# Closing norm of a two-layer decoder step: row sums on TensorE, one store queue

## The chip, the cores and the metric

One core of a Trainium2 chip runs the whole kernel. The metric is the device time of one launch in microseconds (us), as the median of several runs; lower is better. The engines are TensorE (PE, its weight loads listed apart as PEld), VectorE (DVE), ScalarE (ACT), GpSimd (POOL) and SyncE (SP, which only issues transfers here).

## The reference, cut to what matters

The kernel computes one inference step of a two-layer decoder for 256 prompt tokens and 64 sample tokens (8 sequences of 8), with 1024 features each: attention, then gated linear attention, each followed by a mixture of 64 experts. What the change touches is the very last step, after the experts of layer 1:

```python
x = x + g2 * moe(hffn, ...)
return rms_norm(x, final_g), ...

def rms_norm(x, g):
    y = xf * lax.rsqrt(jnp.mean(xf * xf, axis=-1, keepdims=True) + NORM_EPS)
    return (y * g).astype(x.dtype)
```

So each of the 320 tokens needs the sum of its 1024 squares, one root, one reciprocal, and then a product with its own factor and with the row `final_g`. The outputs are `y_prompt` (256 x 1024, float32) and `y_sample` (64 x 1024).

## The kernel before, in words

The residual stream x is kept in on-chip memory as `xT`, features on partitions: 8 chunks (`KC`) of 128 features by 320 tokens. Tokens come in three tiles (`TILES`): 128 prompt tokens, 128 more, and the 64 sample tokens. The expert sums `acct` have tokens on partitions, so at the end of a layer they are turned back chunk by chunk.

The closing stage is `final` (L2218), called from `moe` at L2145. Its PE program (L2233 to L2245) runs over the chunks m = 0 to 7. `back` (L2153) turns chunk m of `acct` with two transposes (L2165) into the one bank of PSUM or the other; at m = 0 and m = 4 `back_sample` (L2147) turns the sample tokens of four chunks first (L2150). `gated_back` on DVE (L2168) multiplies by the gate and adds to `xT` (L2179; for the sample tokens L2174 and L2177), and counts up `x_full`. Behind the `back` of chunk m, PE runs `turned(m - 1)` (L2235): three transposes (L2238), one a tile, which turn the finished chunk so that tokens are on partitions, in the two-bank tensors `ybank`, `pair[1]` and `pair[0]`. The order on PE is thus back 0, back 1, turned 0, back 2, turned 1 and so on to back 7, turned 6, turned 7. `back` of chunk m waits for x of chunk m - 2 (it writes the bank that DVE read), `turned(m)` for x of chunk m.

When four chunks are turned, ACT squares each tile's half and sums it along the row in the same instruction (L2256, two halves by three tiles, the result in `stt`). After the second half DVE adds the two halves (L2270), ACT takes the root (L2259), DVE the reciprocal (L2272). Then three tiles go three ways. Tile 0: one DVE instruction scales by the token's factor and by `g_row` (L2275), and SP stores it (L2291). Tile 2, the sample tokens: ACT scales it (L2263), POOL multiplies by `g_row` (L2283) and issues its store (L2285). Tile 1: ACT scales it behind tile 2 (L2263), DVE multiplies by `g_row` (L2277), SP stores it (L2291). SP then waits for its two stores, POOL for its own.

`g_row` was loaded long before, through the ring of weight slots (L301). The helper `sums` of the other norms of the kernel (L344) sums squares over partitions by products with `ones`, with a 32-column block of ones as the stationary operand. `ada_fold` (L508) and the router (L1602) are other places of the kernel that the prediction takes durations from, and so are the product of two expert-sum parts (L1132), the attention's transposes (L693), the squares of the other norms (L342) and the subtraction at L2108.

## Time and profile before

| | before |
|---|---|
| median of 3 runs | 1496.29 us (1495.95 to 1497.87) |
| the profiled execution, its own time | 1501.47 us |
| its span in the trace | 1499.9 us |
| PE busy | 1443.8 us, 96% of the span, 8392 instructions |
| DVE busy | 439.0 us, 29% |
| ACT busy | 322.0 us, 21% |
| POOL busy | 50.7 us, 3% |
| share of PE in the chain that ended last | 92% |
| TensorE clock granted, mean | 0.985 of full |
| read and written over the span | 499.16 MB and 11.01 MB |

Times inside the trace are counted from the start of the span. A product of two float32 operands shows as two instructions of PE (and two weight loads), a transpose as one. PE's instructions are pipelined, so their listed durations overlap; what one costs in a row of its like is the distance of the starts. In the notation of a PE row, `128*64 128x128` is a stationary operand of 128 partitions by 64 columns and a moving one of 128 by 128.

### The profile page before, as it was taken

To read this page: it belongs to the slowest core of one execution; us is meant where nothing else is said; L and a number is where in the kernel's file an instruction comes from. 1 tells how busy PE (TensorE), PEld (TensorE's weight loads), DVE (VectorE), ACT (ScalarE), POOL (GpSimd) and SP (SyncE) were. 2 spreads that over 40 slices of the span, in tenths; PEclk is the share of its full clock that TensorE was granted. 3 is DMA by queue.
4 is the path that set the end of the run, shared out by engine and by line. 5 is a ranking of instruction groups with operands and counts; after the bars stand their busy time and mean duration, and the time that the engine had idled before them with its cause. 6 is when DMAs were issued, how large, how long until landed. Compare 5 with 4: busy or idle time off the path is not lost.

```text
span 1499.9 us, 21008 instructions
## 1 busy us (share of the span) xinstructions
PE 1443.8 (96%) x8392; PEld 729.0 (49%) x8392; DVE 439.0 (29%) x1146; ACT 322.0 (21%) x752; POOL 50.7 (3%) x86
## 2 busy tenths in 40 slices
PE   6998999999999999999999999999999999999996
PEld 2344666544444445444465455564444454444443
DVE  2126525221221312221352243442122212222113
ACT  3024414111111111111262222321111111111113
POOL 0100302000000000000100010010000000000000
PEclk9999999999999999999999997999999999999998
DMA  9878506999999999999952252189999999999991
GB/s 399 358 309 363 212 14 242 426 377 428 423 423 427 425 424 425 426 424 425 426 230 80 112 208 87 49 346 403 404 423 425 423 427 426 424 426 426 424 419 51
DMA packets 47459, 509.61 MB, mean 340 GB/s; under 512 B 5728, under 2 KB 6000, under 8 KB 8160
## 3 DMA queue, kind: packets, MB, share of 16 engines
q1 hardware_dynamic: 26352, 364.33, 58.3%
q10 hardware_dynamic: 17280, 125.84, 20.3%
q0 software_dynamic: 3728, 18.07, 3.2%
q8 instruction: 69, 1.13, 0.3%
q14 instruction: 30, 0.25, 0.0%
HBM read 499.16 MB, written 11.01 MB: 340 GB/s over the span
## 4 chain that ended last, share of the span: by engine, by line
PE 92%; ACT 3%; DVE 2%; DMA 2%; issue 1%; ACTq 0%; SPq 0%; DVEq 0%
PE bank L1933 27%; PE banks L1982 14%; PE banks L1835 10%; PE banks L430 5%; PE ybank L1863 4%; PE banks L1072 4%; PE banks L1863 3%; PE bank L1865 3%; PE bank L491 2%; PE banks L673 2%; PE banks L1100 2%; DMA s_gu_ring<-in_ada_w_dram 2%; PE ybank L1627 1%; PE banks L1627 1%; PE banks L1077 1%; PE bank L1959 1%
## 5 line engine op out<-in xcount | busy, mean ns | idle before, releaser
L1933 PE MATMUL bank<-s_gu_ring,s_hbuf 128*32 128x512 f32 (+1 forms) x2752 | 409.4, 593 | 0.9 <-DVE s_hbuf L2063 0.9
L1933 PEld LDWEIGHTS bank<-s_gu_ring,s_hbuf 128*32 128x32 f32 (+1 forms) x2752 | 127.4, 119 | 273.6 <-issue 273.6
L1982 PE MATMUL banks<-s_dn_ring,s_hTs 128*32 128x512 f32 (+1 forms) x1376 | 211.5, 596 | 3.8 <-issue 3.8
L2108 DVE TENSOR_TENSOR s_ylo<-banks,s_yhi 128x512 fp32r<-128x512 f32 x116 | 80.2, 692 | 334.6 <-ACT s_yhi L2024 334.6
L1835 PE MATMUL banks<-s_sel,s_htok 128*128 128x512 f32 (+2 forms) x640 | 149.2, 381 | 0.5 <-issue 0.5
L1835 PEld LDWEIGHTS banks<-s_sel,s_htok 128*128 128x128 f32 x640 | 109.9, 188 | 60.7 <-issue 44.4
L2024 ACT CAST s_yhi<-banks 128x512 fp32r<-128x512 f32 x116 | 68.0, 586 | 308.5 <-PE banks L1982 308.5
L1982 PEld LDWEIGHTS banks<-s_dn_ring,s_hTs 128*32 128x32 f32 (+1 forms) x1376 | 58.8, 119 | 125.4 <-issue 125.4
L2103 DVE SCALAR_TENSOR_TENSOR s_hh<-s_sg,s_wsl,bank 128x256 f32<-128x256 f32 x58 | 27.9, 480 | 298.6 <-ACT s_sg L2015 298.6
L2015 ACT ACTIVATE s_sg<-bank 128x256 f32<-128x256 f32 x58 | 22.3, 385 | 376.8 <-PE bank L1933 376.8
L2063 DVE COPY s_hbuf<-banks 128x512 f32<-128x512 f32 (+1 forms) x60 | 40.4, 674 | 100.4 <-PE banks L1835 100.4
L1072 PE MATMUL banks<-s_gu_ring,s_hbuf 128*128 128x512 f32 x128 | 55.9, 593 | 0.5 <-DVE s_rs L1366 0.5
L1998 ACT COPY s_hbuf<-banks 128x512 f32<-128x512 f32 (+1 forms) x60 | 34.4, 573 | 60.1 <-PE banks L1835 60.1
L673 PE MATMUL banks<-s_gu_ring,s_hbuf 128*128 128x512 f32 x96 | 42.4, 597 | 1.2 <-DMA s_gu_ring<-in_wqkv_dram 1.2
L1863 PE MATMUL ybank<-s_yhi,s_gt 128*128 128x512 f32 x112 | 40.1, 438 | 0.0
L430 PE MATMUL banks<-s_qk,s_gu_ring 128*128 128x320 f32 x128 | 38.1, 462 | 1.0 <-ACT s_qk L1303 1.0
L1072 PEld LDWEIGHTS banks<-s_gu_ring,s_hbuf 128*128 128x128 f32 x128 | 24.2, 191 | 29.1 <-issue 28.2
L430 PE MATMUL banks<-s_hbuf,s_gu_ring 128*128 128x320 f32 x128 | 37.4, 456 | 0.8 <-DVE s_hbuf L969 0.8
L491 PE MATMUL bank<-s_gu_ring,s_condT 128*32 128x512 f32 x256 | 34.6, 666 | 2.5 <-DMA s_gu_ring<-in_ada_w_dram 2.5
L2019 ACT COPY s_hTs<-bank 128x256 f32<-128x256 f32 x58 | 21.6, 373 | 68.7 <-PE bank L1959 47.0
L1863 PE MATMUL ybank<-s_ylo,s_gt 128*128 128x512 f32 x112 | 35.4, 397 | 0.0
L1863 PE MATMUL banks<-s_yhi,s_gt 128*128 128x512 f32 x112 | 35.2, 395 | 0.0
(423 smaller groups left out, 1460.2 us busy)
## 6 DMA issues: line engine op xcount, KB each, us to landing
s_gu_ring<-in_moe_up_dram SPq DMA_DIRECT2D x128, 2048.0 KB, 17.5
s_dn_ring<-in_moe_wd_dram ACTq DMA_DIRECT2D x120, 1024.0 KB, 17.6
s_gu_ring<-in_ada_w_dram SPq DMA_DIRECT2D x24, 2048.0 KB, 14.1
s_gu_ring<-in_win_dram SPq DMA_DIRECT2D x6, 2048.0 KB, 15.3
s_dn_ring<-in_moe_wd_dram SPq DMA_DIRECT2D x8, 1024.0 KB, 19.2
s_gu_ring<-in_wqkv_dram SPq DMA_DIRECT2D x3, 2048.0 KB, 21.7
s_gu_ring<-in_wo_dram SPq DMA_DIRECT2D x2, 2048.0 KB, 12.3
s_gu_ring<-in_shared_up_dram SPq DMA_DIRECT2D x2, 2048.0 KB, 12.8
```

The lines of the kernel that those rows point to most:

```text
L430: last = pe.matmul(b[:, 0:T], item(slot)[:, k, (m % 4) * P:(m % 4 + 1) * P], src[:, k, :], start=(k == 0), stop=(k == KC - 1))
L491: last = pe.matmul(ada_bank(n)[32 * j:32 * j + 32, :], condT[:, k, lo:lo + 32], item(s)[:, k, :], start=(x == 0 and kk == 0), stop=(ends_g ...
L673: last = pe.matmul(b[:, :], hT[:, k, t0:t0 + P], item(slots[cch])[:, k, :], start=(k == 0), stop=(k == KC - 1))
L1072: last = pe.matmul(b[:, :], hT[:, k, t0:t0 + P], w[:, k, :], start=(k == 0), stop=(k == KC - 1))
L1835: last = pe.matmul(b[:, width * x:width * x + width], w[:, m * P:(m + 1) * P], sel[:, s, 0:width], start=(n == 0), stop=(n == 4))
L1863: last = pe.matmul(acc[(t, half)], g[:, t * P:(t + 1) * P], y[:, half, :], start=(p == 0 and y is yhi), stop=False)
L1865: last = pe.matmul(bank[6][:, :], g[:, 320 - 64 * half:448 - 64 * half], y[:, half, :], start=(p == 0 and y is yhi and half == 0), stop=False)
L1933: last = pe.matmul(W0[o:o + n, :], tokens_of(p, k)[:, o:o + n], w[:, k, :, :], start=(k == 0), stop=(k == KC - 1))
L1982: last = pe.matmul((W1, W2)[half][o:o + n, :], hTs[:, f, o:o + n], dn_ring[:, dn_of[(l, r)][0], w0:w0 + 512], start=(f == 0), stop=(f == 1))
L2024: act.copy(yhi[:, half, :], (W1, W2)[half]).then_inc(S["y_high"], 1)
L2063: dve.tensor_copy(fill_target(q, f), fill_source(q, f)).then_inc(S["fill_dve"], 1)
L2108: dve.tensor_tensor(ylo[:, half, :], (W1, W2)[half], yhi[:, half, :].bitcast(F32), ALU.subtract).then_inc(S["y_low"], 1)
```

## The change

In `final`, the squares and their sums move. ACT now squares each chunk of `xT` as soon as x of that chunk is there (8 instructions of 128x320), into a buffer `sq` that lies in the first two slots of the ring of down weights. PE sums the squares over the partitions: for each chunk and tile one float32 product with the squares as the stationary operand (128x128, or 128x64 for the sample tokens) and one column of ones as the moving operand, which leaves one column for each chunk in PSUM. These products are put into PE's loop ahead of back 3 (chunk 0), back 5 (chunks 1 and 2) and back 7 (chunks 3 and 4), and between turned 6 and turned 7 (chunks 5, 6 and 7). DVE adds up the eight columns (two reductions, one for the two prompt tiles, one for the sample tile). On tile 1 the product with `g_row` comes first, in two halves, the first behind the last x and the second behind turned 7; ACT then scales it from on-chip memory. Tile 2 is done by DVE in one instruction behind tile 0. SP issues all three stores, in the order tile 0, tile 1, tile 2. POOL has no work left here, and the clearing of `stt` at L2267 is gone.

```diff
-                    final(c, l, i, acct, gate)
+                    old_down = dn_ring[:, 0:2, :].rearrange("p s n -> p (s n)")
+                    final(c, l, i, acct, gate, old_down[:, 0:KC * T].rearrange("p (k t) -> p k t", t=T))
...
+            row_sum = bank[6][:, 256:256 + 3 * KC].rearrange("p (t m) -> p t m", m=KC)
...
+                def row_sums(m):
+                    pe.wait_ge(N["sq_full"], KC * i + m + 1)
+                    for t, (t0, tn) in enumerate(TILES):
+                        last = pe.matmul(row_sum[0:tn, t, m:m + 1], sq[:, m, t0:t0 + tn], ones[:, 0:1], start=True, stop=True)
+                    return last
+
                 for m in range(KC):
+                    if m in (3, 5, 7):
+                        pe.wait_ge(N["x_full"], KC * (i - 1) + m - 1)
+                        for k in range(max(m - 4, 0), m - 2):
+                            row_sums(k)
                     back(pe, l, i, acct, m)
                     if m:
                         turned(m - 1)
+                pe.wait_ge(N["x_full"], KC * i)
+                row_sums(5)
+                row_sums(6)
+                row_sums(7).then_inc(N["sum_psum"], 1)
                 turned(KC - 1)
...
             @block.scalar
             def _(act):
                 act.activation(spare[:, i:i + 1], cc("eps"), ACT.Sqrt)
-                for half in range(2):
-                    act.wait_ge(E["x_psum"], 4 * (half + 1))
-                    for t, (t0, tn) in enumerate(TILES):
-                        n = 3 * half + t
-                        if n >= 2:
-                            act.wait_ge(N["sq_full"], KC * i + n - 1)
-                        act.activation(junk[0:tn, n % 2, :], out[t][0:tn, half, :], ACT.Square,
-                                       accum_out=stt[0:tn, half, t:t + 1]).then_inc(N["sq_full"], 1)
+                for m in range(KC):
+                    act.wait_ge(N["x_full"], KC * (i - 1) + m + 1)
+                    act.activation(sq[:, m, :], xT[:, m, :], ACT.Square).then_inc(N["sq_full"], 1)
                 act.wait_ge(N["part_full"], i + 1)
-                act.activation(stt[:, 3, :], stt[:, 2, :], ACT.Sqrt, scale=1.0 / D, bias=cc("eps")).then_inc(N["root_full"], 1)
+                act.activation(stt[:, 0, 0:2], stt[:, 0, 0:2], ACT.Sqrt, scale=1.0 / D, bias=cc("eps")).then_inc(N["root_full"], 1)
+                act.wait_ge(N["part_full"], i + 2)
+                act.activation(stt[0:NS, 0, 2:3], stt[0:NS, 0, 2:3], ACT.Sqrt, scale=1.0 / D, bias=cc("eps")[0:NS, :]).then_inc(N["root_full"], 1)
+                act.wait_ge(E["gained"], 1)
                 act.wait_ge(N["rstd_full"], i + 1)
-                for t in (2, 1):
-                    tn = TILES[t][1]
-                    act.activation(yt[0:tn, t, :], flat_out(t), ACT.Copy, scale=stt[0:tn, 2, t:t + 1]).then_inc(E["scaled"], 1)
+                act.activation(yt[:, 1, :], yt[:, 1, :], ACT.Copy, scale=stt[:, 1, 1:2]).then_inc(E["scaled"], 1)
 
             @block.vector
             def _(dve):
-                dve.memset(stt[:, :, :], 1.0).then_inc(E["y_full"], 1)
                 gated_back(dve, l, gate, add)
-                dve.wait_ge(N["sq_full"], KC * i + 6)
-                dve.tensor_tensor(stt[:, 2, :], stt[:, 0, :], stt[:, 1, :], ALU.add).then_inc(N["part_full"], 1)
+                slot_in[g_slot].wait(dve, g_in)
+                dve.wait_ge(E["x_psum"], KC // 2)
+                dve.tensor_tensor(yt[:, 1, 0:512], out[1][:, 0, :], g_row[:, 0:512], ALU.mult)
+                dve.wait_ge(N["sum_psum"], 2 * i + 1)
+                dve.tensor_reduce(stt[:, 0, 0:2], row_sum[:, 0:2, :], AX.X, ALU.add).then_inc(N["part_full"], 1)
+                dve.tensor_reduce(stt[0:NS, 0, 2:3], row_sum[0:NS, 2:3, :], AX.X, ALU.add).then_inc(N["part_full"], 1)
+                dve.wait_ge(E["x_psum"], KC)
+                dve.tensor_tensor(yt[:, 1, 512:1024], out[1][:, 1, :], g_row[:, 512:1024], ALU.mult).then_inc(E["gained"], 1)
                 dve.wait_ge(N["root_full"], i + 1)
-                dve.reciprocal(stt[:, 2, :], stt[:, 3, :]).then_inc(N["rstd_full"], 1)
+                dve.reciprocal(stt[:, 1, 0:2], stt[:, 0, 0:2]).then_inc(N["rstd_full"], 1)
+                dve.wait_ge(N["root_full"], i + 2)
+                dve.reciprocal(stt[0:NS, 1, 2:3], stt[0:NS, 0, 2:3]).then_inc(N["rstd_full"], 1)
                 dve.wait_ge(N["rstd_full"], i + 1)
-                slot_in[g_slot].wait(dve, g_in)
-                dve.scalar_tensor_tensor(yt[:, 0, :], flat_out(0), stt[:, 2, 0:1], g_row, ALU.mult, ALU.mult).then_inc(E["y_full"], 1)
-                dve.wait_ge(E["scaled"], 2)
-                dve.tensor_tensor(yt[:, 1, :], yt[:, 1, :], g_row, ALU.mult).then_inc(E["y_full"], 1)
-
-            @block.gpsimd
-            def _(pool):
-                slot_in[g_slot].wait(pool, g_in)
-                pool.wait_ge(E["scaled"], 1)
-                pool.tensor_tensor(yt[0:NS, 2, :], yt[0:NS, 2, :], g_row[0:NS, :], ALU.mult).then_inc(E["sample_full"], 1)
-                pool.wait_ge(E["sample_full"], 1)
-                stored.up(pool.dma_start(a["y_sample"].rearrange("b t d -> (b t) d"), yt[0:NS, 2, :]), 16)
+                dve.scalar_tensor_tensor(yt[:, 0, :], flat_out(0), stt[:, 1, 0:1], g_row, ALU.mult, ALU.mult).then_inc(E["y_full"], 1)
+                dve.wait_ge(N["rstd_full"], i + 2)
+                dve.scalar_tensor_tensor(yt[0:NS, 2, :], flat_out(2), stt[0:NS, 1, 2:3], g_row[0:NS, :], ALU.mult, ALU.mult).then_inc(E["y_full"], 1)
 
             @block.sync
             def _(sp):
-                for t in range(2):
-                    sp.wait_ge(E["y_full"], 2 + t)
-                    sp.dma_start(a["y_prompt"][0, P * t:P * t + P, :], yt[:, t, :]).then_inc(E["out"], 16)
-
-                sp.wait_ge(E["out"], 32)
+                sp.wait_ge(E["y_full"], 1)
+                sp.dma_start(a["y_prompt"][0, 0:P, :], yt[:, 0, :]).then_inc(E["out"], 16)
+                sp.wait_ge(E["scaled"], 1)
+                sp.dma_start(a["y_prompt"][0, P:2 * P, :], yt[:, 1, :]).then_inc(E["out"], 16)
+                sp.wait_ge(E["y_full"], 2)
+                sp.dma_start(a["y_sample"].rearrange("b t d -> (b t) d"), yt[0:NS, 2, :]).then_inc(E["out"], 16)
+
+                sp.wait_ge(E["out"], 48)
```

## Rows read from the trace of the kernel before

**Rows 1.** Chain of waits, closing stage: start us, us, what ended last

```profile
1487.54 0.33 PE ybank L2238
...
1488.13 1.84 ACT s_junk L2256 x6
...
1489.99 0.18 DVE s_stt_f L2270
...
1490.19 0.30 ACT s_stt_f L2259
...
1490.52 0.19 DVE s_stt_f L2272
...
1490.73 1.11 ACT s_yt L2263
...
1492.87 2.53 DVE s_yt L2277
```

**Rows 2.** Timeline of the loop: start us, us, engine, line, op, [idle before <-releaser]

```profile
1482.81 1.03 DVE L2179 SCALAR_TENSOR_TENSOR s_xT<-bank,s_mod,s_xT 128x256 f32<-128x256 f32 x2 [0.47 <-PE bank L2165]
1482.83 0.25 PEld L2165 LDWEIGHTS bank<-s_cst,s_hbuf 128*128 128x128 f32 x2
...
1483.83 0.32 PEld L2150 LDWEIGHTS banks<-s_cst,s_hbuf 64*128 64x128 f32 x4 [0.20 <-issue]
...
1484.71 0.25 PEld L2165 LDWEIGHTS bank<-s_cst,s_hbuf 128*128 128x128 f32 x2
...
1485.65 0.33 PE L2238 MATMUL ybank<-s_cst,s_xT 128*128 128x128 f32 x1 [0.46 <-DVE s_xT L2179]
...
1486.46 1.03 DVE L2179 SCALAR_TENSOR_TENSOR s_xT<-bank,s_mod,s_xT 128x256 f32<-128x256 f32 x2 [0.47 <-PE bank L2165]
```

**Rows 3.** Timeline of the tail, GpSimd's product and SP's two stores

```profile
1491.98 2.34 POOL L2283 TENSOR_TENSOR s_yt<-s_yt,s_gu_ring 64x1024 f32<-64x1024 f32 x1 [504.08 <-ACT s_yt L2263]
1492.04 3.73 SPq L2291 DMA_DIRECT2D out_y_prompt_dram<-s_yt  x2
```

**Rows 4.** Timeline of PE alone, around 169 us, ada_fold and what follows

```profile
169.22 1.08 PE L508 MATMUL bank<-s_cst,s_asb 128*128 128x32 f32 x8 [0.22 <-ACT s_asb L500]
170.13 0.41 PE L740 MATMUL ybank<-s_cst,s_sc 128*128 128x128 f32 x2
```

**Rows 5.** Timeline of PE alone, around 231 us, the router and what follows

```profile
231.50 1.09 PE L1602 MATMUL ybank<-s_hbuf,s_router 128*64 128x64 f32 x16
232.53 0.66 PE L1613 MATMUL bank<-s_cst,s_hbuf 128*128 128x128 f32 x4
```

**Rows 6.** Timeline of PE alone, around 807 us, products of 16 moving columns

```profile
806.90 0.65 PE L1132 MATMUL banks<-s_work 128*64 128x16 f32 x16
807.39 0.31 PE L1134 MATMUL banks<-s_work 128*64 128x64 f32 x2
```

**Rows 7.** Weight loads of L508: duration ns min/median/max, first and last start us

```profile
L508 PEld LDWEIGHTS bank<-s_cst,s_asb x48: 186/192/192, 23.0 to 170.0; 128*128 128x128 f32 x48
```

**Rows 8.** Timeline of PE alone, transposes while the granted clock was halved

```profile
129.10 2.39 PE L693 MATMUL ybank<-s_cst,s_qkv 128*128 128x128 f32 x10 [1.46 <-issue]
```

**Rows 9.** Groups of instructions, shapes apart: busy us, mean ns of one

```profile
L342 ACT ACTIVATE s_sq<-s_xT 128x320 f32<-128x320 f32 x24 | 10.1, 462 | 41.4 <-DVE s_xT L406 29.9 <-PE banks L348 9.9 <-PE ybank L348 1.4
...
L2108 DVE TENSOR_TENSOR s_ylo<-banks,s_yhi 128x512 fp32r<-128x512 f32 x116 | 80.2, 692 | 334.6 <-ACT s_yhi L2024 334.6
...
L2275 DVE SCALAR_TENSOR_TENSOR s_yt<-ybank,s_stt_f,s_gu_ring 128x1024 f32<-128x1024 f32 x1 | 1.3, 1284 | 0.0
```

**Rows 10.** Windows: length, PE, PEld, DVE, ACT, POOL busy, PEclk, DMA share, GB/s

```profile
1488.10:1491.00 2.90, 0.00 (x0) 0.00 (x0) 0.61 (x3) 2.40 (x8) 0.00 (x0) 1.00 0.00 0
...
1493.00:1493.25 0.25, 0.00 (x0) 0.00 (x0) 0.25 (x1) 0.00 (x0) 0.25 (x1) 0.50 1.03 426
...
1496.00:1496.25 0.25, 0.00 (x0) 0.00 (x0) 0.00 (x0) 0.00 (x0) 0.00 (x0) 0.50 1.16 246
...
1498.75:1499.00 0.25, 0.00 (x0) 0.00 (x0) 0.00 (x0) 0.00 (x0) 0.00 (x0) 0.50 0.17 66
```

More of the change, by code:

```diff
@@ L2216, in _, with final @@
                     ada_mod(dve, n)
-        def final(c, l, i, acct, gate):
-            E = {n: sem("final_" + n) for n in ("x_psum", "scaled", "sample_full", "y_full", "out")}
+        def final(c, l, i, acct, gate, sq):
+            E = {n: sem("final_" + n) for n in ("x_psum", "gained", "scaled", "y_full", "out")}
             g_slot, g_in = stream_next(lambda dst: [(dst[:, 0:2, :].rearrange("p k n -> p (k n)"),
@@ L2223, in final @@
             g_row = item(g_slot)[:, 0:2, :].rearrange("p k n -> p (k n)")
-            junk = sb("junk", [P, 2, 512], c=c)
-            stt = sb("stt_f", [P, 4, 3], c=c)
+            stt = sb("stt_f", [P, 2, 3], c=c)
             yt = sb("yt", [P, 3, D], c=c)
```

## The prediction

> **What bounds the kernel now.** The chain that ended last is read first: 92% of it is PE, and nothing of the change lies there, for the expert passes up to about 1479 us are as they were. So only the last 21 us can move, and in these I read the chain again in order of time [rows 1]. The last turned 7 starts at 1487.54. Behind it PE has nothing left and the work hops: ACT's six squares (1.84), DVE's addition (0.18), ACT's root (0.30), DVE's reciprocal (0.19), ACT's scaling of two tiles (the 1.11 shown and the rest of the second, up to 1492.85), DVE's product with the weight (2.53), the second store. The reader is to see that the longest link is that last product: 128x1024 in 2.53 us. It ran beside POOL's product of the sample tile, 1491.98 to 1494.32 [rows 3], while a DVE instruction of the same size that has no such company took 1.284 (L2275 in [rows 9]).
>
> Second, the timeline of the loop [rows 2]. DVE's last two x end at 1487.49. PE and DVE hand over to each other: back 3 starts at 1482.83, and x 3, the second of the pair that ends at 1483.84, starts 0.48 earlier, at 1483.36. So from the start of a back to the start of its x it is 0.53, and to its end 1.01. Whatever is put ahead of a back goes into this loop, unless PE had to wait there anyway.
>
> Third, the stores. SP issued at 1492.04 and at 1495.42 (3.73 for both, the last issue taking 0.35) [rows 3]. The first store ran at 426 GB/s [rows 10], beginning some 0.83 behind its issue. The second shared the engines with POOL's store of the sample tile and got 246 GB/s at a full share of busy time [rows 10]; the last bytes moved shortly before 1499.0, and the span ends at 1499.9, 0.95 later.
>
> **Part 1, the row sums on PE.** 8 chunks by 3 tiles by 2 instructions: 48 instructions and 48 weight loads. No row has a moving operand of one column behind float32 weights, so the price is bounded. The nearest row is the fold: 128x128 float32 weights, 32 moving columns, 8 instructions between 169.22 and 170.13: 0.114 each [rows 4]. For 64 weight columns it is the router: 16 between 231.50 and 232.53, 0.064 each [rows 5]. Here the time goes with the weight columns, as the moving ones are few. Below stands L1132, 16 in 0.49 or 0.031 each [rows 6], which has 64 weight columns and writes alternating halves of the partitions; above, a weight load that nothing overlaps, 0.192 as the row lists it [rows 7]. I take 0.114 and 0.064, because shape and type are those of the change in all but the moving columns: a chunk costs 4 x 0.114 + 2 x 0.064 = 0.58, all eight 4.7.
>
> The Trainium skill (TensorE: Matmul & The Clock Gate, LDWEIGHTS) gives a load as its columns over 1.2 GHz, an estimate of 107 ns for 128 and 53 ns for 64. The same page's section on the back-to-back gap gives about 25 ns as the floor for 1 to 64 moving columns; by it the eight chunks would take 48 x 0.025 = 1.2. The rows side with the first of the two.
>
> The loop, worked on from the rows of before. Chunk 0 ahead of back 3: ACT's table is loaded and x 0 is there, its square (0.46 [rows 9]) ends near 1482.7, so PE does not wait. Back 3 goes from 1482.83 to 1483.41, x 3 ends at 1484.42. Turned 2 runs 1483.63 to 1483.96, and the sample turning starts 0.20 behind that, at 1484.16 instead of 1483.83 [rows 2]: 0.33 later, and x 4 with it, from ready at 1485.65 to 1485.98. Back 5 was at 1484.71, is at 1485.04 by that shift, and has chunks 1 and 2 (1.17) ahead of it: 1486.21. Here PE had stood idle for x 4 until 1485.65, so only part is new. X 5 ends at 1487.22; turned 4 and back 6 (1486.76) give x 6 at 1487.77; turned 5 waits for x 5 and ends at 1487.54. Chunks 3 and 4 (1.17) put back 7 at 1488.71 and x 7 at 1489.72. **The loop ends 2.23 later** (1489.72 for 1487.49).
>
> **Part 2, from x 7 to the factor.** PE waits for x 7, then 3 x 0.58 = 1.75: 1489.76 to 1491.51. The square of chunk 7 (to 1490.22) is ready before its product. With about 0.2 until the result is seen, DVE reduces 1491.70 to 1492.05 (two at about 0.18, taken from the small DVE instruction of rows 1; a read of PSUM may make it 0.2). Turned 7, behind the sums, is seen 0.59 from its start (1487.54 to 1488.13 before [rows 1]): 1492.10. So its delay costs little, since DVE is reducing. The second half of the product on tile 1 takes 0.69 (L2108 in [rows 9], same size and one operand in PSUM), to 1492.79; the first half sits behind x 7, 1489.74 to 1490.43, while PE sums, and costs nothing; without that cover it would be 0.69. The two roots (0.30 each [rows 1], 1491.90 to 1492.50) lie beside the product. Two reciprocals: 1493.18. The removed clearing of `stt` was in DVE's slack and is worth nothing.
>
> **Part 3, the outputs.** Tile 0 on DVE: 1.284, to 1494.48. Tile 1's scaling on ACT, about 1.10, from 1493.03 to 1494.13: hidden behind tile 0, since SP stores tile 0 first. Tile 2 on DVE: about 1.25 at 64 partitions, since cost goes with the row's length; to 1495.73. What is queued behind SP's waits are the stores alone. They are issued at 1494.51, 1494.86 and 1495.76. Tile 0's data start 0.83 behind their issue, at 1495.34. All three, 1.31 MB, at 426 GB/s: 3.08, to 1498.42. So the stores follow one another without a gap, and what the sample tile's late issue costs is nothing: alone it would end at 1495.76 + 0.83 + 0.62 = 1497.2. With the 0.95 the span ends at **1499.37, against 1499.9: 0.5 less**.
>
> **The sum** against the profiled execution (1501.47, span 1499.9): the loop +2.23; from x 7 to the end 12.41 before, 9.65 after, -2.76; together -0.53. The profiled execution is 5.2 above the median of the runs; the closing stage is the same work in both, so I carry the difference over unchanged: 1496.29 - 0.5 = 1495.8. A measurement of this kernel tells about 0.2% from no change, 3.0 us.
>
> **The rivals.**
> - **Cheap sums.** If a one-column product costs 0.031, a chunk is 0.19. Then chunk 0 hides before x 2, chunks 1 and 2 hide in the idle time before x 4, chunks 3 and 4 put x 7 at 1487.86, and the sums are ready 0.92 behind it (bound by the last square, 0.46) and not 1.98: 1.86 and 1.06 less, 1499.37 - 2.92 = 1496.45, so -3.45 and **1492.8**. For it: the rows of L1132 [rows 6]. Against: those have half the weight columns and alternate halves of the array, and the fold with few moving columns still took 0.114. The skill's 25 ns floor, named above, would come out here. Chance 0.12.
> - **Dear sums.** If the weight load hides nothing, at 0.192 for 128 columns and some 0.14 for 64, a chunk is 1.05: eight chunks are 3.7 dearer, and in this part of the loop all of it is on the path. 1499.37 + 3.7 = 1503.1: +3.2, **1499.5**. It decides from 0.13 a load on, where the 0.5 is eaten. The same side has the clock: PE's granted clock stayed at 1.00 until 1491.00 although PE had stopped at 1488.1 [rows 10], and the transposes did not lower it. With one column moving at a time it may fall to 0.5 (1.2 GHz) earlier; ten transposes at that level took 2.39 [rows 8], about double. If it falls before the last three chunks, these and turned 7 cost 2.0 more, +1.5; if before chunks 3 and 4, 3.6 more, +3.1. Together 0.11, of which 0.08 above 0.2%.
> - **The stores do not run at full rate.** The second store of before got 246 GB/s beside POOL's. I blame the company of POOL's many small packets, not two stores at once. If it were two stores at once, tiles 1 and 2 would take 0.79 MB / 246 = 3.2 for 1.85: +1.35, in all +0.8, **1497.1**. Chance 0.10.
> - **The forecast**, 0.67: -1.3 to +0.3, since 0.10 for 0.114 in a load gives 0.6 back and a sample tile priced like a full one takes 0.8; with the spread of a median, 1494.3 to 1497.3.
>
> **How the numbers follow.** Forecast 1495.8. The range runs to 1492.9 on the side of cheap sums and to 1498.4 on the other side, which leaves out most of the dear sums. Faster by over 0.2% has the cheap sums and a little of the forecast by noise, 0.13; slower by over 0.2% has 0.08; within 0.2% the rest, 0.79.
>
> **What would show it.** In the changed kernel's timeline: the 6 instructions of a chunk 0.58 apart from start to start; x 7 ending near 1489.7, if the passes before end where they did; the first reduction near 1491.7; no DVE instruction above 1.3 us; stores issued about 4.8, 5.1 and 6.0 behind x 7, 1.31 MB moved at about 426 GB/s without a dip to 246. The prediction is wrong if x 7 ends below 1488 (cheap sums) or above 1491 (dear sums), if the granted clock is 0.5 before turned 7, or if DVE waits for squares and not for PE.

## The result, and the profile after

The changed kernel takes 1502.55 us, the median of 15 runs (1499.13 to 1504.19), and the kernel before 1498.13 (1495.95 to 1502.68, 15 runs beside them). The two medians are 4.4 apart. The ratio of the two sets of runs is 1.0022, 95% interval 1.0013 to 1.0032: slower by about 3.3 us. The forecast was a gain of 0.5, and the 1502.55 lies above the range.

| | before | after |
|---|---|---|
| profiled execution / its span | 1501.47 / 1499.9 us | 1503.69 / 1501.9 us |
| PE busy, instructions | 1443.8 us, 8392 | 1447.5 us, 8440 |
| DVE / ACT / POOL busy | 439.0 / 322.0 / 50.7 us | 439.0 / 320.7 / 47.0 us |
| TensorE clock granted, mean | 0.985 | 0.985 |

The closing stage begins at another time in every execution, since the 1475 us before it vary: in the profiles below, between 1474.29 and 1479.19. So I count from one fixed place, the first of the eight products of `keep_awake` (L411) that run directly ahead of L2150, to the end of the span, and call that **closing time**. It splits into three: the loop (to the end of x 7), from there to SP's first store issue, and from that issue to the end of the span. It was 20.71 us before and is 23.72 after, +3.01. (The span itself grew by only 2.0, because this stage happened to begin 1.0 earlier.)

| step, us | before | forecast | after |
|---|---|---|---|
| start to the end of x 7 | 8.30 | 10.53 | 11.19 |
| x 7 to the first store issue | 4.55 | 4.79 | 6.62 |
| first store issue to the end | 7.86 | 4.86 | 5.91 |
| closing time | 20.71 | 20.18 | 23.72 |

The timeline of the changed kernel, closing stage (start us, us, engine, line, operation; in brackets the idle time before and what ended it), to be set beside [rows 1 to 3]:

```profile
1478.18 1.05 PE L411 MATMUL bank<-s_cst 128*128 128x128 f32 x8
...
1484.24 1.45 PE L2245 MATMUL bank<-s_cst,s_dn_ring 128*128 128x1 f32 x12
...
1485.63 0.44 PE L2166 MATMUL bank<-s_cst,s_hbuf 128*128 128x128 f32 x2
...
1488.89 0.48 DVE L2180 SCALAR_TENSOR_TENSOR s_xT<-bank,s_mod,s_xT 128x256 f32<-128x256 f32 x1 [1.75 <-PE bank L2166]
1489.29 0.68 DVE L2281 TENSOR_TENSOR s_yt<-banks,s_gu_ring 128x512 f32<-128x512 f32 x1
...
1489.43 3.58 PE L2245 MATMUL bank<-s_cst,s_dn_ring 128*128 128x1 f32 x18 [0.25 <-DVE s_xT L2180]
...
1492.94 0.48 PE L2239 MATMUL ybank<-s_cst,s_xT 128*128 128x128 f32 x1
...
1493.05 0.17 DVE L2283 TENSOR_REDUCE s_stt_f<-bank 128x2 f32<-128x16 f32 x1 [3.08 <-PE bank L2245]
...
1493.25 0.30 ACT L2269 ACTIVATE s_stt_f<-s_stt_f,s_cst 128x2 f32<-128x2 f32 x1 [3.38 <-DVE s_stt_f L2283]
...
1493.88 0.69 DVE L2286 TENSOR_TENSOR s_yt<-banks,s_gu_ring 128x512 f32<-128x512 f32 x1 [0.60 <-PE banks L2239]
1494.49 0.16 DVE L2288 RECIPROCAL s_stt_f<-s_stt_f 128x2 f32<-128x2 f32 x1
...
1494.68 1.28 DVE L2292 SCALAR_TENSOR_TENSOR s_yt<-ybank,s_stt_f,s_gu_ring 128x1024 f32<-128x1024 f32 x1
1494.74 1.15 ACT L2274 ACTIVATE s_yt<-s_yt,s_stt_f 128x1024 f32<-128x1024 f32 x1 [1.00 <-DVE s_stt_f L2290]
1495.88 1.27 DVE L2294 SCALAR_TENSOR_TENSOR s_yt<-banks,s_stt_f,s_gu_ring 64x1024 f32<-64x1024 f32 x1
1495.99 0.35 SPq L2299 DMA_DIRECT2D out_y_prompt_dram<-s_yt  x1
1496.39 0.43 SPq L2301 DMA_DIRECT2D out_y_prompt_dram<-s_yt  x1
1497.17 0.56 SPq L2303 DMA_DIRECT2D out_y_sample_dram<-s_yt  x1
```

Three readings. The 12 products of a pair of chunks start at 1484.24 and the next instruction at 1485.63, so a pair costs 1.39 where 1.17 was forecast. The last 18 go from 1489.43 to 1492.94: 3.51 for a forecast 1.75, or 0.195 each. And DVE waited 3.08 us for them, idle but for L2281 behind x 7. The windows (length; PE, PEld, DVE, ACT, POOL busy; granted clock; DMA share; GB/s) say what the 18 products suffered from, and are to be set beside [rows 10] for the stores:

```profile
1478.18:1489.42 11.24, 10.18 (x84) 8.82 (x82) 6.04 (x14) 6.06 (x13) 0.00 (x0) 1.00 0.01 1
1489.43:1492.94 3.51, 3.51 (x19) 3.42 (x19) 0.54 (x1) 0.45 (x1) 0.00 (x0) 0.54 0.00 0
...
1496.75:1499.25 2.50, 0.00 (x0) 0.00 (x0) 0.40 (x1) 0.00 (x0) 0.00 (x0) 0.50 0.99 392
1499.50:1500.50 1.00, 0.00 (x0) 0.00 (x0) 0.00 (x0) 0.00 (x0) 0.00 (x0) 0.50 1.03 242
...
1499.45:1500.75 1.30, 0.00 (x0) 0.00 (x0) 0.00 (x0) 0.00 (x0) 0.00 (x0) 0.50 0.87 202
```

The granted clock was 1.00 up to x 7 and 0.54 over the 18 products, with PE listed as busy all the time. Before, it had stayed at 1.00 for nearly 3 us behind PE's last instruction [rows 10]. And there is a dip to 242 GB/s again, which the prediction said would be gone, now at the end and with nothing of POOL's in it. A window counts each packet at its start. The last row has the whole store of the sample tile, to the end of its last packet: 0.26 MB in 1.30 us, 202 GB/s.

### The profile page after: what moved, and what is told of

Read it like the earlier page. It is cut to its first block, busy times and chain, and to the rows that moved or that the text cites. A ratio compares the mean times of both kernels' runs of the same rounds, so it can differ in the third digit from the quotient of the medians.

```text
span 1501.9 us, 21105 instructions
## 1 busy us (share of the span) xinstructions
PE 1447.5 (96%) x8440; PEld 735.3 (49%) x8440; DVE 439.0 (29%) x1149; ACT 320.7 (21%) x748; POOL 47.0 (3%) x84
## 4 chain that ended last, share of the span: by engine, by line
PE 90%; DMA 4%; ACT 2%; DVE 2%; issue 1%; SPq 0%; DVEq 0%; ACTq 0%
PE bank L1933 26%; PE banks L1982 13%; PE banks L1835 10%; PE banks L430 5%; PE banks L1072 4%; PE ybank L1863 4%; PE banks L1863 3%; PE bank L1865 3%; DMA s_gu_ring<-in_ada_w_dram 3%; PE banks L673 2%; PE banks L1100 2%; PE bank L491 2%; DMA s_gu_ring<-in_moe_up_dram 1%; PE ybank L1627 1%; PE banks L1627 1%; PE banks L1077 1%
## 5 line engine op out<-in xcount | busy, mean ns | idle before, releaser
L1863 PE MATMUL banks<-s_ylo,s_gt 128*128 128x512 f32 x112 | 34.9, 393 | 0.0
## 6 DMA issues: line engine op xcount, KB each, us to landing
s_gu_ring<-in_ada_w_dram SPq DMA_DIRECT2D x24, 2048.0 KB, 13.5
```

The source lines that it names most:

```text
L1863: last = pe.matmul(acc[(t, half)], g[:, t * P:(t + 1) * P], y[:, half, :], start=(p == 0 and y is yhi), stop=False)
```

## The experiments

Closing time is what the single profiles are compared by: of kernels profiled twice, before repeats to 0.05 us, e3 to 0.01, e2 to 0.05, and the changed kernel itself to 0.7. The clock's fall lies in the first quarter microsecond with a granted clock under 1.00, placed inside it by that quarter's mean.

| kernel | closing | to x 7 | x 7 to issue | issue to end | PE's end | clock falls | the fall against PE's end |
|---|---|---|---|---|---|---|---|
| before | 20.71 | 8.30 | 4.55 | 7.86 | 8.90 | 11.9 | +3.0 |
| before again (e12) | 20.66 | 8.29 | 4.56 | 7.81 | 8.89 | 13.5 | +4.6 |
| changed | 23.72 | 11.19 | 6.62 | 5.91 | 15.67 | 11.5 | -4.2 |
| changed again (e1) | 24.40 | 11.68 | 6.84 | 5.88 | 16.37 | 9.8 | -6.6 |
| 64 moving columns (e2) | 22.93 | 11.73 | 5.29 | 5.91 | 14.87 | 16.7 | +1.9 |
| the same again (e8) | 22.88 | 11.71 | 5.30 | 5.87 | 14.86 | 17.7 | +2.8 |
| old sums, new outputs (e3) | 18.59 | 8.30 | 4.55 | 5.74 | 8.90 | 11.9 | +3.0 |
| the same again (e9) | 18.60 | 8.30 | 4.55 | 5.75 | 8.90 | 10.6 | +1.7 |
| new sums, old outputs (e4) | 24.70 | 11.19 | 5.70 | 7.81 | 15.45 | 11.8 | -3.6 |
| no sums of tile 2 (e5) | 20.20 | 9.71 | 4.57 | 5.92 | 12.14 | 11.0 | -1.1 |
| tile 1 stored in halves (e6) | 19.28 | 8.29 | 4.56 | 6.43 | 8.90 | 11.1 | +2.2 |
| tile 0 in halves (e7) | 17.91 | 8.30 | 4.02 | 5.59 | 8.90 | 11.2 | +2.3 |
| sums grouped by tile (e10) | 21.90 | 10.83 | 5.19 | 5.88 | 13.87 | 13.9 | +0.05 |
| 16 moving columns (e11) | 22.27 | 11.31 | 5.06 | 5.90 | 14.22 | 14.3 | +0.07 |

All in us; PE's end and the fall are counted from the start of the closing stage too. The first four experiments were timed together, beside 20 runs of before (median 1498.53).

**e1, the changed kernel again**, with no edit.

> The changed kernel once more, unchanged. Closing time is counted from the first keep-awake product (L411) to the end of the span: 20.7 us before, 23.7 us in the first profile of the changed kernel, where PE's clock fell from 1.00 to 0.50 about 0.4 us into the last 18 one-column products (3.58 us for them). Theory (the one-column products leave the array so idle that the clock falls during them): it falls again before turned 7, the 18 products take between 2.2 (no fall) and 3.6 us, closing time 22.0 to 23.7. Rival (the fall at that place was chance): the clock stays at 1.00 to the end of turned 7, 18 products in 2.2 us, closing time about 22.

Measured: 1504.76 us (4 runs), 1.0052 [1.0035, 1.0069] against before. In this execution the clock fell 9.8 us after the start, inside the pair of chunks 3 and 4, so the loop was longer too (11.68) and the last 18 products took 3.73 at a clock of 0.50. Both lie above what was expected of the theory (3.6 and 23.7). So the lower clock is no accident of one profile, but where it begins varies, and with it the closing time, by 0.7.

**e2, 64 columns of ones in the moving operand** instead of one. The chip does more in each product, and the numbers in the first column of each are the same.

```diff
-            row_sum = bank[6][:, 256:256 + 3 * KC].rearrange("p (t m) -> p t m", m=KC)
+            row_sum = bank[6][:, 256:256 + 3 * 80].rearrange("p (t m) -> p t m", m=80)
...
-                        last = pe.matmul(row_sum[0:tn, t, m:m + 1], sq[:, m, t0:t0 + tn], ones[:, 0:1], start=True, stop=True)
+                        last = pe.matmul(row_sum[0:tn, t, m:m + 64], sq[:, m, t0:t0 + tn], ones[:, 0:64], start=True, stop=True)
...
```

> The row sums with 64 moving columns of ones in place of one (the later columns are written over), all else as in the changed kernel. Theory (the price of a product is its weight load, and the clock falls because so few columns move): the products of the loop stay at 0.12 us each, but the clock holds at 1.00 through turned 7, so the last 18 take 2.2 us and not 3.6, turned 7 is 0.3 shorter, closing time about 22.0. Rival (the fall has nothing to do with the columns): clock 0.50 in the last 18 again, 3.6 us, closing time 23.7 or more. Second rival (the moving columns have a price of their own): 0.15 us or more each in the loop.

Measured: 1501.15 (10 runs), 1.0020 [1.0008, 1.0031]. A window of its last 18 products:

```profile
1489.45:1492.00 2.55, 2.54 (x19) 2.14 (x19) 0.55 (x1) 0.46 (x1) 0.00 (x0) 1.00 0.00 0
```

They take 2.55 at a clock of 1.00, where one column took 3.51 at 0.54. The loop is 0.54 longer, since a pair costs 1.59, and still the closing time is 0.8 to 1.5 shorter. So the clock is a real part of the loss, and the weight of each product is another: even at full clock these products are dearer than forecast. At 1.59 / 12 = 0.13 an instruction they lie between the 0.12 of the theory and the 0.15 of its second rival.

**e3, old sums with the new outputs.** The squares by ACT as before, and everything behind the factor as in the change. For tile 1's two half products to run between the squares, ACT takes tile 1 first in its second half.

```diff
-                    for t, (t0, tn) in enumerate(TILES):
-                        n = 3 * half + t
+                    for x, t in enumerate(((0, 1, 2), (1, 0, 2))[half]):
+                        t0, tn = TILES[t]
+                        n = 3 * half + x
...
+                slot_in[g_slot].wait(dve, g_in)
+                dve.wait_ge(N["sq_full"], KC * i + 2)
+                dve.tensor_tensor(yt[:, 1, 0:512], out[1][:, 0, :], g_row[:, 0:512], ALU.mult)
+                dve.wait_ge(N["sq_full"], KC * i + 4)
+                dve.tensor_tensor(yt[:, 1, 512:1024], out[1][:, 1, :], g_row[:, 512:1024], ALU.mult).then_inc(E["gained"], 1)
                 dve.wait_ge(N["sq_full"], KC * i + 6)
...
```

> Half of the change alone: the squares stay on ACT's reads of PSUM as before (second half in the order tile 1, 0, 2), but tile 1 gets its final weight ahead of the root, tile 2 is done by DVE and SP issues all three stores. Theory (the loss is all in the row sums, the outputs' half is a gain): x 7 as before, factor known 3.2 us behind x 7, first store 4.55 us behind x 7 as before, the stores then follow one another; closing time 18.7 to 19.3, that is 1.5 to 2.0 below the 20.7 of before and 4 to 5 below the changed kernel. Rival (one queue for the stores costs what the shorter chain brings): closing time 20.5 or more.

Measured: 1497.25 (10 runs), 0.9998 [0.9989, 1.0008], and a closing time 2.12 below before's, all of it behind the first store issue. Its timeline:

```profile
1485.15 0.60 ACT L2257 ACTIVATE s_junk<-banks 128x512 f32<-128x512 f32 x1 [1.28 <-PE banks L2238]
...
1485.87 0.69 DVE L2273 TENSOR_TENSOR s_yt<-banks,s_gu_ring 128x512 f32<-128x512 f32 x1 [0.76 <-ACT s_junk L2257]
...
1487.01 0.16 DVE L2275 TENSOR_TENSOR s_stt_f<-s_stt_f 128x3 f32<-128x3 f32 x1 [0.45 <-ACT s_junk L2257]
```

Tile 1's second half product ends at 1486.56, before ACT has squared the last tile: here it is free. The windows of the stores show the dip at the end as in the changed kernel, 395 GB/s and then 186:

```profile
1489.75:1492.50 2.75, 0.00 (x0) 0.00 (x0) 0.47 (x1) 0.00 (x0) 0.00 (x0) 0.50 0.98 395
1492.75:1493.50 0.75, 0.00 (x0) 0.00 (x0) 0.00 (x0) 0.00 (x0) 0.00 (x0) 0.50 0.84 186
```

**e4, new sums with the old outputs.**

```diff
-                act.wait_ge(E["gained"], 1)
-                act.wait_ge(N["rstd_full"], i + 1)
-                act.activation(yt[:, 1, :], yt[:, 1, :], ACT.Copy, scale=stt[:, 1, 1:2]).then_inc(E["scaled"], 1)
+                act.wait_ge(N["rstd_full"], i + 2)
+                act.wait_ge(E["x_psum"], KC)
+                for t in (2, 1):
+                    tn = TILES[t][1]
+                    act.activation(yt[0:tn, t, :], flat_out(t), ACT.Copy, scale=stt[0:tn, 1, t:t + 1]).then_inc(E["scaled"], 1)
...
```

> The other half alone: row sums on PE by one-column products as in the changed kernel, outputs as before (ACT scales tiles 2 and 1, POOL weights and stores tile 2, DVE weights tile 1 last). Theory (the row sums cost 2.9 us in the loop and more behind x 7): x 7 ends 11.2 us behind the first keep-awake product instead of 8.3; factor 4.0 behind x 7 with a clock that falls, 2.6 without, against 3.2 before; closing time 23.0 to 24.5. Rival (the row sums are about even and the loss is in the outputs): closing time 20 to 21.5.

Measured: 1502.93 (5 runs), 1.0035 [1.0016, 1.0053]; closing +3.99. Together with e3: **the sums cost 4.0, the outputs bring 2.1.** That adds up to +1.9, and the changed kernel shows +3.0 to +3.7. The rest is in the step from x 7 to the issue, 6.62 against e4's 5.70. The rows name it. In e4 DVE takes the first reciprocal 0.53 behind its first reduction (1493.76 and 1494.29); in the changed kernel 1.44 behind it (1493.05 and 1494.49), because the half product L2286 stands in between and waits for turned 7, at the lower clock. No run moved the reciprocals ahead of it.

```profile
1493.76 0.17 DVE L2282 TENSOR_REDUCE s_stt_f<-bank 128x2 f32<-128x16 f32 x1 [3.46 <-PE bank L2245]
...
1494.29 0.17 DVE L2285 RECIPROCAL s_stt_f<-s_stt_f 128x2 f32<-128x2 f32 x1 [0.30 <-ACT s_stt_f L2269]
...
1495.92 2.33 POOL L2299 TENSOR_TENSOR s_yt<-s_yt,s_gu_ring 64x1024 f32<-64x1024 f32 x1 [508.15 <-ACT s_yt L2276]
...
1496.81 2.53 DVE L2293 TENSOR_TENSOR s_yt<-s_yt,s_gu_ring 128x1024 f32<-128x1024 f32 x1 [0.84 <-ACT s_yt L2276]
```

The last two rows are the pair that [rows 1, 3] showed: DVE's product in 2.53 beside POOL's. In the changed kernel both are gone, and no DVE instruction of the tail is above 1.28. That POOL is what made the 2.53 is argued from this: no run has this product of DVE's without POOL's beside it.

**e5, without the products of tile 2** (the factor of the sample tokens is then not that of their own sum). It prices the 64-column weights in this order.

```diff
-                    for t, (t0, tn) in enumerate(TILES):
+                    for t, (t0, tn) in enumerate(TILES[0:2]):
...
```

> The changed kernel without the row sums of tile 2 (left out: the sample tokens' own sums; their factor is taken from the sums of tile 0): 4 instructions a chunk, all with 128 weight columns, where there were 6. In the changed kernel a chunk costs 0.74 us at full clock. Theory (a load of 64 columns behind one of 128 costs as much, 0.12 us, so the prediction's 0.064 was the mis-sized part): a chunk costs 0.49 us at full clock. Rival (0.064 was right and 128 columns cost 0.15): 0.61 us. In either case the clock falls before turned 7 or does so later than the last product, as phase has it.

Measured: 1496.96 in one run; closing 3.52 below the changed kernel's. Its PE timeline, the pair of chunks 1 and 2 and what follows:

```profile
1482.96 0.95 PE L2245 MATMUL bank<-s_cst,s_dn_ring 128*128 128x1 f32 x8
1483.78 0.42 PE L2166 MATMUL bank<-s_cst,s_hbuf 128*128 128x128 f32 x2
```

8 instructions with 128 weight columns in 0.82, or 0.41 a chunk, which is below both of the expected values, 0.49 and 0.61. The whole pair has 12 in 1.39, so tile 2's four add 0.57, 0.14 each. In this order the smaller weights are the dearer ones, where [rows 5] gave 0.064. The 0.82 is no plain 0.10 each. In the trace the second product of such a run starts 0.03 behind the first and each further one 0.11 behind the one before it, which is the 0.114 of the forecast.

**e6, old sums, new outputs, tile 1's store split by partitions** (e3 and this edit), to see what sets the rate.

```diff
-                sp.dma_start(a["y_prompt"][0, P:2 * P, :], yt[:, 1, :]).then_inc(E["out"], 16)
+                sp.dma_start(a["y_prompt"][0, P:P + NS, :], yt[0:NS, 1, :]).then_inc(E["out"], 16)
+                sp.dma_start(a["y_prompt"][0, P + NS:2 * P, :], yt[NS:P, 1, :]).then_inc(E["out"], 16)
...
```

> The kernel with old sums and new outputs, with tile 1 stored as two transfers of 64 partitions each in place of one of 128. There the stores' data moved from 1489.8 to 1493.5 of the span: about 410 GB/s for tiles 0 and 1, then about 190 GB/s in the last 0.7 us, the sample tile's. Theory (a store that reads 64 partitions moves at half the rate): from tile 1 on about 200 GB/s, the data take 1.2 us longer, closing time 19.8 in place of 18.6. Rival (the low rate is the run-out of whatever store comes last, or its small size): tile 1 still at 410 GB/s, closing time 18.6 to 18.8.

Measured: 1498.02 in one run; closing +0.69 against e3. In the trace each store of 64 partitions is 64 packets of 4 KB and 16 of a few bytes, which close it. From 1490.50 up to 1493.13 exactly the 192 large packets of tile 0 (128) and of the first half (64) start, and tile 0's 16 small ones:

```profile
DMA packets 208, 0.79 MB, mean 299 GB/s; under 512 B 16, under 2 KB 16, under 8 KB 208
```

So in these windows the first is that half (partitions 0 to 63), the second is the other half (64 to 127), of which 58 packets start before its first closing one, and the third is the sample tile (partitions 0 to 63) with the last 6 of them:

```profile
1491.86:1493.13 1.27, 0.00 (x0) 0.00 (x0) 0.00 (x0) 0.00 (x0) 0.00 (x0) 0.50 0.95 206
1493.13:1493.81 0.68, 0.00 (x0) 0.00 (x0) 0.00 (x0) 0.00 (x0) 0.00 (x0) 0.50 1.08 349
1493.81:1494.44 0.63, 0.00 (x0) 0.00 (x0) 0.00 (x0) 0.00 (x0) 0.00 (x0) 0.50 0.96 364
```

The first half ran at 206 GB/s with the engines listed as busy, as the theory has it, but the second ran at 349 and the sample tile at 364, where the same tile had 202 in the changed kernel. The loss is about half of what was expected. So 64 partitions as such do not set the rate, and what made the first half slow and not the two stores behind it is open. The Trainium skill (SBUF — State Buffer, "Door 1: The DMA port swizzle") says that partitions 0 to 63 reach 8 of 16 ports, with an asymptote of about 218 GB/s against 436 for all. The 206 and the 202 agree. The 349 and 364 do not, and the measurement decides. The same page ("Can I just issue two DMAs to hit both halves?") says that two stores at partitions 0 and 64 serialize. Here they did follow one another, as the count of packets shows.

**e7 and e9, timed together** beside 23 runs of before (median 1497.61), as were the single runs of e5 and e6. e9 is e3 once more, e7 is e3 with tile 0's product and store in two halves of 512 columns.

```diff
-                dve.scalar_tensor_tensor(yt[:, 0, :], flat_out(0), stt[:, 2, 0:1], g_row, ALU.mult, ALU.mult).then_inc(E["y_full"], 1)
+                for h in range(2):
+                    dve.scalar_tensor_tensor(yt[:, 0, 512 * h:512 * h + 512], out[0][:, h, :], stt[:, 2, 0:1], g_row[:, 512 * h:512 * h + 512],
+                                             ALU.mult, ALU.mult).then_inc(E["y_full"], 1)
...
```

> The kernel with old sums and new outputs once more, with more rounds, since its closing time was 18.6 us against 20.7 before but its interval of the first time held no change. Theory (the 2.1 us saved at the end are real and nothing before them changed): median 1 to 3 us below before, interval of the ratio wholly or nearly below 1. Rival (what the end saves is lost elsewhere): ratio at 1.000.

> The kernel with old sums and new outputs, with tile 0 scaled and stored in two halves of 512 features, so that the first store is issued some 0.6 us earlier. Theory (behind the factor the end is set by the first issue and then by the stores one after another): first issue 0.6 us nearer to the factor, closing time 18.0 against 18.6. Rival (rows of 2 KB move more slowly, or SP's issues of 0.4 us each become the bound): closing time 18.6 or more.

Measured: e9 1495.63 (12 runs), 0.9983 [0.9973, 0.9992]; e7 1495.52 (12 runs), 0.9985 [0.9976, 0.9994]. Both are faster than before. e9's first timing, as e3, gave 0.9998, whose interval just overlaps this one; the closing times 18.59 and 18.60 say that the kernel is 2.1 ahead in its own stage both times. e7's first issue comes 0.53 earlier and its closing time is 0.7 lower still, too little for its median to show.

**e8, e10, e11 and e12, one run each on one chip.** e8 is e2 again and e12 is before again. e10 keeps one moving column and puts the products of a group in another order: first all with 128 weight columns, then all with 64. e11 is e2 with 16 columns of ones.

```diff
-                    for t, (t0, tn) in enumerate(TILES):
-                        last = pe.matmul(row_sum[0:tn, t, m:m + 1], sq[:, m, t0:t0 + tn], ones[:, 0:1], start=True, stop=True)
...
+                    for tiles in ((0, 1), (2,)):
+                        for m in ms:
+                            for t in tiles:
+                                t0, tn = TILES[t]
+                                last = pe.matmul(row_sum[0:tn, t, m:m + 1], sq[:, m, t0:t0 + tn], ones[:, 0:1], start=True, stop=True)
...
```

> The row sums with 64 moving columns once more, one look. The first time PE's clock held at 1.00 through turned 7 and the last 18 products took 2.55 us, where three kernels with one-column products had 3.3 to 3.7 us and a clock of 0.50 before turned 7. Theory (the few columns make the clock fall): it holds again, 18 products in 2.5 to 2.6 us, closing time 22.9. Rival (luck of the phase): 0.50 before turned 7, closing time 24 or more.

> One-column row sums as in the changed kernel, but where two or three chunks are summed together, the products of tiles 0 and 1 of all of them come first and those of tile 2 (64 weight columns) behind them. From the first product of a pair of chunks to the next back it was 1.39 us in the changed kernel with 12 instructions and 0.82 without tile 2's 4, so tile 2's cost 0.14 each. Theory (0.14 is the price of going over from 128 to 64 weight columns and back, and 64 columns in a row cost 0.064): 0.82 + 4 x 0.064 + one change of 0.15, about 1.23 us a pair. Rival (0.14 is the price of each such instruction): 1.39 us again.

> Row sums with 16 moving columns in place of one or 64. Theory (what keeps the clock is how much of the time columns move): at 16 columns of some 0.12 us a product moves little more than at one, so the clock falls to 0.50 before turned 7 as with one column, closing time 23.7 to 24.7. Rival (any product of more than one column is enough, or the fall has to do with single columns as such): 1.00 through turned 7, closing time 22.3 to 22.9.

> The kernel before, unchanged, for a second closing time on this chip: 20.7 us if the first was typical (20.5 to 20.9); sample store and tile 1's store together at about 250 GB/s again.

e8 measured: 1501.32, closing 22.88, the last 18 products in 2.54 at a clock of 1.00. e12: 1497.61, closing 20.66. Both repeat their first profiles. Over the 3 us in which e12's sample tile and tile 1 are stored the mean is 243 GB/s, as was expected of both together:

```profile
1492.00:1495.00 3.00, 0.00 (x0) 0.00 (x0) 0.00 (x0) 0.00 (x0) 0.00 (x0) 0.50 0.86 243
...
1491.75:1493.00 1.25, 0.00 (x0) 0.00 (x0) 0.00 (x0) 0.00 (x0) 0.00 (x0) 0.50 1.08 197
1493.50:1494.25 0.75, 0.00 (x0) 0.00 (x0) 0.00 (x0) 0.00 (x0) 0.00 (x0) 0.50 0.95 388
```

But the two halves of it differ, and they are two stores, one behind the other. In before the same stretch, 1495.75 to 1497.00, has packets of POOL's queue (q0) alone:

```profile
DMA packets 60, 0.25 MB, mean 197 GB/s; under 512 B 0, under 2 KB 0, under 8 KB 60
...
q0 software_dynamic: 60, 0.25, 108.2%
```

So the 246 of [rows 10] (1496.00 to 1496.25) was the sample tile by itself. Tile 1's first packet starts at 1497.01, 1.6 behind its issue at 1495.42, and it then ran at 426 as tile 0 did.

e10: 1498.39, closing 21.90. In its PE timeline the pair takes 1.20 (1480.77 to 1481.97) and the last 18 take 1.84:

```profile
1480.77 1.27 PE L2248 MATMUL bank<-s_cst,s_dn_ring 128*128 128x1 f32 x12
1481.97 0.44 PE L2166 MATMUL bank<-s_cst,s_hbuf 128*128 128x128 f32 x2
...
1486.18 1.91 PE L2248 MATMUL bank<-s_cst,s_dn_ring 128*128 128x1 f32 x18 [0.84 <-ACT s_dn_ring L2267]
1488.02 0.33 PE L2239 MATMUL ybank<-s_cst,s_xT 128*128 128x128 f32 x1
```

The same 12 instructions in another order are 0.19 cheaper, as the theory has it (1.23), and close to the forecast's 1.17. With e5's 0.82 for the eight and 0.064 for each of the four [rows 5] the sum is 1.08. The grouped pair goes to the small weights and back once and lies 0.12 above that sum, the mixed pair twice and lies 0.31 above it. So going there and back costs 0.12 to 0.19. Starts of single products show where. First four of the mixed order, answers to narrow windows (a row begins with the earliest product that still runs), then three of e10:

```profile
1484.50 0.25 PE L2245 MATMUL bank<-s_cst,s_dn_ring 128*128 128x1 f32 x1
1484.68 0.28 PE L2245 MATMUL bank<-s_cst,s_dn_ring 128*64 128x1 f32 x2
1484.76 0.40 PE L2245 MATMUL bank<-s_cst,s_dn_ring 128*64 128x1 f32 x2
1484.88 0.27 PE L2245 MATMUL bank<-s_cst,s_dn_ring 128*128 128x1 f32 x1
...
1481.65 0.22 PE L2248 MATMUL bank<-s_cst,s_dn_ring 128*64 128x1 f32 x1
1481.73 0.31 PE L2248 MATMUL bank<-s_cst,s_dn_ring 128*64 128x1 f32 x3
1481.79 0.26 PE L2248 MATMUL bank<-s_cst,s_dn_ring 128*64 128x1 f32 x2
```

The first product with small weights stands 0.18 behind the last with large ones, against 0.11 between large ones. Between two small ones it is 0.08 at first and 0.06 later, and back to a large one 0.12. The waits between chunks, which e10 also lacks, cost nothing: in e5 they are there and the products keep their 0.11. The router of [rows 5], where the 0.064 came from, changes its size once behind 16. e10's order has a price of its own. Its last 18 wait for the last square, and PE stands idle for 0.84 before them.

e11: 1500.67, closing 22.27, a pair in 1.43, the last 18 in 2.30 at a clock of 1.00. But its clock fell right behind PE's end, as e10's did, not 2 to 3 us later as with 64 columns. Its closing time is the one expected of the rival, but it doesn't tell the theories of the clock apart.

## Why the prediction was wrong

Of the 3.54 us between forecast (-0.53) and profile (+3.01), the loop has 0.66, the step to the first store 1.83, the stores 1.05.

**The price of a row sum: the failed step was the 0.064 for 64 weight columns.** 0.114 for 128 columns was right (0.11), 0.064 much too little (0.14 on average), because the row it was taken from has one size of weights and the change alternates two. Chunk 0 made x 3 0.11 later than forecast, and a pair cost 1.39 for 1.17. That gives 0.11 + 2 x 0.22 = 0.55 of the loop's 0.66. For the last three chunks at full clock one and a half pairs give 2.09, but in e2 and e11 the last 18 took 0.15 more than one and a half pairs (2.54 for 2.39, 2.30 for 2.15). My estimate is 2.24 for the 1.75, so 0.49 more. e10 shows the cause by the order. The Trainium skill (TensorE: Matmul & The Clock Gate, LDWEIGHTS) gives an estimate of 53 ns for 64 columns. The 0.06 between small weights in e10 agrees, the mixed order does not. The Trainium skill (TensorEngine Tiling (Array Packing), Key Properties) says that a change of tiling mode drains TensorE. A surcharge per change would fit that. That the two sizes of weights are two modes here, and that a drain is what happens, no run shows. "Cheap sums" is refuted: a product cost 0.10 to 0.14 on average, and only the second of a run stood 0.03 behind the first. The 25 ns that the prediction quotes from the Trainium skill (TensorE: Matmul & The Clock Gate, Back-to-back issue gap) is no nearer.

**The clock: a rival at too low a chance.** It was named, with +1.5 if it fell before the last three chunks and +3.1 if before chunks 3 and 4, and shared a chance of 0.11 with the dear sums. In the profile it fell just behind x 7, and the 18 products took 3.51 for the 2.24 of a full clock: 1.27 of the 1.83. The argument against it was that the clock had held through the transposes and for 3 us without any work [rows 10]. That was a fact of another order of work. Before this fall PE had run the eight products of `keep_awake`, then transposes and one-column products, 11.5 us in all, and was listed as busy for 10.18 of the 11.24 up to x 7, so the busy share did not announce it. In the four profiles with one-column sums chunk by chunk (changed, e1, e4, and e5, which has one size of weights) the clock fell 1.1 to 6.6 us before PE's end; in the two with 64 columns, and in all with the old sums, 1.7 to 4.6 behind it. That the 64 columns kept it, in two profiles of two, is shown. That one column as such loses it is not: e10 has one column and held its clock to PE's end, and e11 with 16 columns held it no longer than that. The moment of the fall also varies between executions of one kernel, by 1.7 us in the changed one and by 1.6 in before.

Counted from the start of the closing stage the table reads differently: the fall comes at 9.8 to 11.8 with the one-column sums chunk by chunk, and at 10.6 to 13.5 with the old sums, where PE had stopped at 8.9. So beside the old sums the one-column products did not clearly bring the fall forward. They made PE's work longer without putting the fall off, and the work ran into it. e10's 13.9 and e11's 14.3 are close to before's 13.5, and only the 64 columns (16.7 and 17.7) are well beyond. Whether e10's order does anything for the clock is open, with one profile of it.

**From the sums to the factor: right in kind.** The forecast had 1.48 from the first reduction to the end of the reciprocals, measured 1.64. In e2, at full clock, it was 1.29, so the clock has some 0.35 here too, by way of turned 7. It had the half product of 0.69 on the path. What it didn't see is that this was a choice: in e3 the same product hides behind ACT, in e4 the factor is there 0.9 sooner without it.

**The outputs: right, and the only gain.** The prediction put DVE's 2.53 down to POOL beside it. Both rows go with the change and come back with e4, which fits and does not prove it. SP's second and third issue stand 0.40 and 1.18 behind the first, for a forecast 0.35 and 1.25. The tile 1 scaling (1.15) was hidden behind tile 0.

**The stores: the failed step was 1.31 MB at 426 GB/s, and the reading of the 246.** From the first packet to the end of the last the data took 3.9 for 3.08, and the span ended 1.1 behind them for 0.95. The prediction read the 246 as two stores sharing the engines and blamed POOL's small packets. There was no sharing: it was the sample tile alone, in packets of 4 KB as tile 1's, and tile 1 came behind it. From SP's queue, with POOL idle, the same tile alone had 202. So neither POOL nor company is the cause, and the tile stands last, where nothing hides it. The rival (two stores at once) had 1.35 more in this step, for a measured 0.8 and another 0.2 at the end: the right sign by the wrong mechanism. What makes this store slow is open, since e6 has a slow store of 64 partitions and two fast ones. Open is also why the end follows the last packet's end by 1.1 in the changed kernel and in e3 and by 0.9 in before and e12.

**Noise.** The median of before, 1496.29 in 3 runs, is 1498.13 in 15. Of the 6.75 between forecast and median, 1.84 is this. The closing stage has 3.5 to 4.2 (the changed kernel and e1), and the 0.7 to 1.4 that are left are not accounted for.

**The best version** keeps half of the change: old sums, new outputs. It takes the 2.1 us of the outputs and pays nothing on PE. With tile 0 in halves (e7) the closing time is lower by another 0.7, the lowest here.

## What to carry to other kernels

Before taking the price of a product from another place in a trace, look at what stands around it: size of weights, order, and whether the sizes alternate; where they must, put equal ones together. Work moved to TensorE because "it has room" is paid for where TensorE and another engine hand over to each other, and it can end under a lower clock, which a busy share does not show. Try the parts of a change alone: here one half was worth 2 us and the other cost 4.

## What the runs showed that was not expected

- Products with weights of 64 columns cost more (0.14 us on average) than those with 128 (0.11) when the two alternate; in a row of their like they cost 0.06.
- The granted clock went to half, 1.2 GHz, up to 6.6 us before PE's last instruction, with PE listed as busy for nine tenths of the time before the fall and all of the 3.5 us in which it fell (the changed kernel; the 6.6 is e1's). With 64 moving columns in place of one the same program kept 2.4 GHz to PE's end, and its closing time was shorter by 0.8 to 1.5 us though each product was dearer.
- The sample tile's store, 64 partitions, ran at 197 to 212 GB/s when it moved alone (before, e12, the changed kernel, e3), where one from 128 ran at 390 to 426. In e6 the first store of 64 partitions ran at 206 and the two behind it at 349 and 364.
- In before tile 1's store did not share the engines with POOL's. Its data came behind POOL's, 1.6 us after its issue.
